# A fixed quarter of the experts as dense products beside the gathers

## The chip, the cores and the metric

The kernel runs on one core of a Trainium2 chip in one launch. The metric is the time of an execution on the device in microseconds (us). All values are 32-bit floats.

## The reference, cut to what matters

Two transformer layers run over 256 tokens of width 2048: a convolution block with a gated feed-forward, then attention, pooling and a mixture of single-neuron experts. The change touches only the mixture, the last part:

```python
q = (xt @ w_query).reshape(t, 8, 256); q1, q2 = halves of q
s1, s2 = q1 . sub_keys_1, q2 . sub_keys_2          # 128 keys each
v1, i1 = top_k(s1, 16); v2, i2 = top_k(s2, 16)
cand = v1[..., :, None] + v2[..., None, :]          # 16 x 16 pairs
top_s, pos = top_k(cand, 16); expert = i1 * 128 + i2 at pos
gates = softmax(top_s)
a = einsum('thkd,td->thk', expert_u[expert], x)     # 8 heads x 16 picks a token
hid = gelu(a) * gates
out = x_residual + einsum('thk,thkd->td', hid, expert_v[expert])
```

There are 128 x 128 = 16,384 experts. An expert's first key, 0 to 127, is its number divided by 128. The tables expert_u and expert_v have one row of 2048 floats (8 KB) for each expert.

## The kernel before, in words

The layers run stage by stage. Up to the query projection, weights stream in as 292 panels of 1 MB (128 partitions x 2048 floats) that SyncE (SP) loads into a ring of four buffers, `raw` (lines 364 to 369); ScalarE and VectorE split each panel into two parts, and TensorE (PE) multiplies.

The mixture starts when the last panel is used. Tokens lie on the partitions in two tiles of 128. A tile and a head make a *route* (16 routes), with 16 picks, in order of tile and head; four picks make a *group*, 64 groups in all (`ROUTES`, `GROUPS`, `BATCH`, lines 250, 251). One gather brings, for one pick of one route, one table row for each of the 128 partitions: 1 MB.

- **GpSimd (POOL)** issues the gathers in a fixed order: u of pick k, then v of pick k - 6 (`LAG`), as indirect DMAs (`gather_u`, line 441; `gather_v`, line 450). u has 4 buffers, and one comes free when the dot of four picks before is done. v has 8, and they come free four at a time, when TensorE has finished a group (`v_used`).
- **VectorE (DVE)** takes one dot per u buffer (`dot`, line 1282), its product going back into that buffer. Ahead of the third group of each route it works out the whole next route (`route`: the sixteen best keys of both halves, the best pairs, the expert numbers, the gates; lines 1221 to 1269). So a route is worked out in one group of four. After a group's four dots, `hidden` multiplies the activation by the gate.
- **ScalarE (ACT)** takes the gelu of four dots, writes `spread` (16 small copies of an identity, scaled by the hidden values, line 801) and copies each route's expert numbers into v's layout (16 copies, line 790).
- **TensorE** adds a group (`adds`, line 1646): 16 products of spread and v rows into four PSUM banks of the tile. Before the first and after the last group of a tile, `nothing` multiplies zeros (line 1634) to open and close the banks. VectorE then adds the banks to the residual (`result`, line 1322), and SP stores a tile (line 368).

The v rows lie differently from the u rows: partition 32 s + r of the buffer of pick 4 j + q holds token 32 q + r of pick 4 j + s.

```python
for k in range(ROUTES * TOPK + LAG):
    if k < ROUTES * TOPK:
        gather_u(k)
    if k >= LAG:
        gather_v(k - LAG)
```

Of the kernel before, what the change touches and what calls it, by code (L numbers as in the profile page):

```python
# [22 lines left out]
D = 2048  # L23
# [11 lines left out]
SLOTS = PH * TOPK  # L35
RMS_EPS, LN_EPS = 1e-6, 1e-5
# [77 lines left out]

class Counts:
# [39 lines left out]
def two_layers(nc, stream, columns, x, meta, b_out, g_mix_post, g_ffn_post, g_norm2, w_forget,  # L155
# [19 lines left out]

    cols = keep("s_cols", [128, NCOLS])
    ident = keep("s_ident", [128, 128])
    ones = keep("s_ones", [128, 128])
    tri_ones = keep("s_tri_ones", [128, 2 * 128])
    causal = keep("s_causal", [128, 128])  # L180
    group_sb = keep("s_group_w", [128, 4, 2, 256])
    wf_raw = keep("s_wf_raw", [128, KT, HEADS])
# [67 lines left out]
    NU, NV, NW, BATCH, LAG = 4, 8, 4, 4, 6  # L250
    ROUTES, GROUPS = TT * PH, TOPK // BATCH
    Q = 32
    u_slot = [place(f"s_u{i}", [128, D], ring0 + i * 8 * K) for i in range(NU)]
    v_slot = [place(f"s_v{i}", [128, D], ring0 + (NU + i) * 8 * K) for i in range(NV)]
    assert ring0 + (NU + NV) * 8 * K <= S
    P0 = S + 66 * K
    spread = [place(f"s_spread{i}", [128, 4, Q], P0 + i * 512) for i in range(NW)]
    P0 += NW * 512

    def small(name, n, dt=f32):  # L260
        nonlocal P0
        t = place(name, [128, n], P0, dt)
        P0 += (4 * n + 63) // 64 * 64
        return t

    sc = small("s_sc", 2 * NKEYS)
# [4 lines left out]
    cand = small("s_cand", TOPK * TOPK)  # L271
    cand_rest = small("s_cand_rest", TOPK * TOPK)
# [4 lines left out]
    pick = small("s_pick", TOPK * TOPK)  # L277
    chosen = small("s_chosen", 2 * TOPK)
    expert_f = [small(f"s_expert_f{i}", TOPK) for i in range(2)]
    u_index = [small(f"s_u_index{i}", TOPK, u32) for i in range(ROUTES)]  # L280
    v_index = [place(f"s_v_index{i}", [128, 4, GROUPS], S + 33 * K + i * 64, u32) for i in range(ROUTES)]
    gate = [small(f"s_pgate{i}", TOPK) for i in range(2)]
    gsum = small("s_gsum", 4)
    iota_i = small("s_iota_i", TOPK, mybir.dt.int32)
    iota_f = small("s_iota_f", TOPK)
# [3 lines left out]
    assert P0 <= S + 78 * K, P0 - S  # L289
    zeros = place("s_zeros", [128, 128], S + 65 * K)  # L290

    with ExitStack() as ctx:
# [41 lines left out]
        zeros_ready, iota_ready = sem("zeros_ready"), sem("iota_ready")  # L334
# [16 lines left out]
        def _(sp):  # L351
# [7 lines left out]
            with sp.Fori(1, NPANELS // 4) as q:  # L359
                for s in range(4):  # L360


                    sp.wait_ge(panel_used, q * 4 + (s - 4 + 1 + 1))
                    sp.dma_start(raw[s][:, :], panels[bass.ds(q, 1), s].rearrange("a p n -> (a p) n"))\
                        .then_inc(raw_loaded[s], 16)
            for t in range(TT):
                sp.wait_ge(out_ready, t + 1)
                sp.dma_start(out[t * 128:(t + 1) * 128, :], xres[:, t, :]).then_inc(stored, 16)
            sp.wait_ge(stored, 16 * TT)
# [3 lines left out]
        def _(pool):  # L373
# [7 lines left out]
            n.base["pool_step"] = 5  # L381
# [47 lines left out]
            pool.iota(iota_i[:, :], pattern=[[1, TOPK]], base=0, channel_multiplier=0).then_inc(iota_ready, 1)  # L429
            pool.memset(zeros[:, :], 0.0).then_inc(zeros_ready, 1)  # L430
# [4 lines left out]
            def gather_u(k):  # L435
# [5 lines left out]
                pool.indirect_dma_start(u_slot[k % NU][:, :], None, expert_u, index).then_inc(u_loaded[k % NU], 16)  # L441

            def gather_v(k):

                th, slot = divmod(k, TOPK)
                j, q = divmod(slot, 4)
                pool.wait_ge(v_index_ready, th + 1)
                wait(pool, v_used, (k - NV) // 4 + 1)
                index = bass.IndirectOffsetOnAxis(ap=v_index[th][:, q, j:j + 1], axis=0)
                pool.indirect_dma_start(v_slot[k % NV][:, :], None, expert_v, index).then_inc(v_loaded[k % NV], 16)  # L450
# [9 lines left out]
        def _(act):  # L460
# [321 lines left out]
            def route(th):  # L782

                act.wait_ge(gate_max, th + 1)
                act.activation(gate[th % 2][:, :], top[:, :], ACT.Exp, bias=gsum[:, 0:1], accum_out=gsum[:, 1:2])\
                    .then_inc(gate_exp, 1)
                act.wait_ge(expert_ready, th + 1)
                for s in range(4):
                    for q in range(4):
                        ins = act.activation(v_index[th][s * Q:(s + 1) * Q, q, :], expert_f[th % 2][q * Q:(q + 1) * Q, s::4], ACT.Copy)  # L790
# [13 lines left out]

            route(0)
            for g in range(ROUTES * GROUPS):
                th, j = divmod(g, GROUPS)
                if j == 2 and th + 1 < ROUTES:
                    route(th + 1)
                if g:  # L810
                    spreads(g - 1)
                part = slice(j * BATCH, (j + 1) * BATCH)
                act.wait_ge(dot_ready, (g + 1) * BATCH)
                act.activation(gelu[th % 2][:, part], adot[th % 2][:, part], ACT.Gelu_apprx_tanh).then_inc(gelu_ready, 1)  # L814
            spreads(ROUTES * GROUPS - 1)
# [3 lines left out]
        def _(dve):  # L819
# [412 lines left out]
            def best_keys(th, halves):  # L1232

                if 0 in halves:
                    link(dve.tensor_copy(sc[:, :], score[:, th, :]))
                for half in halves:
                    sixteen(val[:, half * TOPK:(half + 1) * TOPK], ind[:, half * TOPK:(half + 1) * TOPK],
                            sc[:, half * NKEYS:(half + 1) * NKEYS], sc_rest[:, :])
# [10 lines left out]
            def pairs_experts(th):  # L1249
# [5 lines left out]
                picks = pick[:, :].rearrange("p (k a) -> p k a", a=TOPK)  # L1255
                for half in range(2):
# [469 lines left out]
```

## Time and profile before

| | us |
|---|---|
| median of 3 runs | 3256.39 |
| lowest and highest | 3250.51, 3256.89 |
| the profiled execution | 3256.63 |
| its span, first to last instruction | 3254.9 |

The span has 38175 instructions. TensorE is busy for 68% of it, VectorE for 56%, ScalarE for 36%, GpSimd for 20%. Memory traffic is 855.36 MB, 543.27 of it on GpSimd's software queue and 310.85 on SP's hardware queue.

How to read it: times are microseconds from the start of the span, means of single instructions in nanoseconds. PE is TensorE's products and PEld its weight loads, which overlap them; a 32-bit product shows as two records. "Busy" is the union of an engine's instructions. Idle time is put down to what ended it (`<-`). PEclk is the granted share of TensorE's clock, and the DMA share is the mean busy share of 16 DMA engines. L1282 is line 1282 of the kernel.

### The profile page before, as it was taken

To read this page: it belongs to the slowest core of one execution; us is meant where nothing else is said; L and a number is where in the kernel's file an instruction comes from. 1 tells how busy PE (TensorE), PEld (TensorE's weight loads), DVE (VectorE), ACT (ScalarE), POOL (GpSimd) and SP (SyncE) were. 2 spreads that over 40 slices of the span, in tenths; PEclk is the share of its full clock that TensorE was granted. 3 is DMA by queue.
4 is the path that set the end of the run, shared out by engine and by line. 5 is a ranking of instruction groups with operands and counts; after the bars stand their busy time and mean duration, and the time that the engine had idled before them with its cause. 6 is when DMAs were issued, how large, how long until landed. Compare 5 with 4: busy or idle time off the path is not lost.

```text
span 3254.9 us, 38175 instructions
## 1 busy us (share of the span) xinstructions
PE 2201.9 (68%) x14110; PEld 1774.7 (55%) x14110; DVE 1827.5 (56%) x2515; ACT 1165.8 (36%) x2115; POOL 654.1 (20%) x557
## 2 busy tenths in 40 slices
PE   7996889999999969999999891222222232222324
PEld 6885679999999969889998780000000010000001
DVE  5896555555554553764445455555555565555553
ACT  2003354444444443344333443333333333333332
POOL 0000000000000000120000016444444444444442
PEclk9998989999999989899999996566666666666566
DMA  5331435555555535334555449999999999999998
GB/s 225 144 142 67 179 119 192 180 188 186 185 189 181 190 119 181 117 130 151 186 180 200 148 165 402 418 414 417 412 416 414 417 414 417 417 414 419 418 417 343
DMA packets 117560, 855.36 MB, mean 263 GB/s; under 512 B 13104, under 2 KB 13104, under 8 KB 13248
## 3 DMA queue, kind: packets, MB, share of 16 engines
q0 software_dynamic: 74656, 543.27, 40.6%
q1 hardware_dynamic: 42800, 310.85, 26.4%
q8 instruction: 47, 0.77, 0.1%
q14 instruction: 57, 0.47, 0.0%
HBM read 851.97 MB, written 2.10 MB: 262 GB/s over the span
## 4 chain that ended last, share of the span: by engine, by line
PE 50%; DMA 21%; DVE 14%; issue 6%; POOL 5%; ACT 3%; DVEq 0%; POOLq 0%; SPq 0%; ACTq 0%
DMA s_u<-in_expert_u,s_u_index 19%; PE bank L1355 13%; PE bank L1357 13%; PE bank L1356 13%; PE bank L1435 7%; DVE s_u L1282 4%; POOL s_u L441 3%; POOL s_v L450 2%; DMA s_v<-in_expert_v,s_v_index 2%; DVE s_w_lo L842 1%; DVE s_yrow L1008 1%; PE bank L1646 1%; ACT s_w_hi L471 1%; DVE s_qrs L1046 1%; ACT s_xs L477 0%
## 5 line engine op out<-in xcount | busy, mean ns | idle before, releaser
L1646 PE MATMUL bank<-s_v,s_spread 128*32 128x512 f32 x2048 | 368.3, 884 | 922.9 <-DMA s_v<-in_expert_v,s_v_index 907.8
L842 DVE TENSOR_TENSOR s_w_lo<-s_raw,s_w_hi 128x2048 fp32r<-128x2048 f32 x259 | 594.7, 2297 | 646.8 <-ACT s_w_hi L471 646.6
L1282 DVE CUSTOM_DVE_ANT_0 s_u<-s_u,s_xn 128x2048 f32<-128x2048 f32 x256 | 584.1, 2291 | 505.6 <-DMA s_u<-in_expert_u,s_u_index 505.0
L1646 PEld LDWEIGHTS bank<-s_v,s_spread 128*32 128x32 f32 x2048 | 93.0, 155 | 1197.9 <-issue 1037.5
L471 ACT ACTIVATE s_w_hi<-s_raw 128x2048 fp32r<-128x2048 f32 x260 | 497.8, 1915 | 652.5 <-PE bank L1357 652.4
L1355 PE MATMUL bank<-s_a_hi,s_w_hi 128*128 128x256 f32 x2560 | 722.5, 282 | 12.8 <-DVE s_w_lo L842 7.8
L1356 PE MATMUL bank<-s_a_lo,s_w_hi 128*128 128x256 f32 x2560 | 722.7, 282 | 0.0
L1357 PE MATMUL bank<-s_a_hi,s_w_lo 128*128 128x256 f32 x2560 | 722.0, 282 | 0.0
L1355 PEld LDWEIGHTS bank<-s_a_hi,s_w_hi 128*128 128x128 f32 x2560 | 486.1, 190 | 17.5 <-DVE s_w_lo L842 10.5
L1357 PEld LDWEIGHTS bank<-s_a_hi,s_w_lo 128*128 128x128 f32 x2560 | 486.8, 190 | 0.0
L1356 PEld LDWEIGHTS bank<-s_a_lo,s_w_hi 128*128 128x128 f32 x2560 | 482.9, 189 | 1.4 <-issue 1.0
L441 POOL DMA_INDIRECT s_u<-in_expert_u,s_u_index x256 | 320.0, 1250 | 773.7 <-DVE s_adot L1282 510.0
L801 ACT ACTIVATE s_spread<-s_ident,s_hid 32x32 f32<-32x32 f32 x1024 | 325.5, 318 | 218.0 <-DVE s_hid L1291 205.6
L450 POOL DMA_INDIRECT s_v<-in_expert_v,s_v_index x256 | 297.2, 1161 | 95.8 <-issue 79.4
L408 POOL MEMSET s_pin<- 128x128 f32 x1 | 0.2, 207 | 1367.6 <-ACT s_pin L603 1367.6
L1435 PE MATMUL bank<-s_a_f,s_raw 128*128 128x272 f32 x1024 | 236.6, 394 | 0.8 <-DVE s_a_f L889 0.8
L1435 PEld LDWEIGHTS bank<-s_a_f,s_raw 128*128 128x128 f32 x1024 | 195.6, 191 | 41.5 <-DVE s_a_f L889 0.9
L916 DVE SCALAR_TENSOR_TENSOR s_cacc<-s_cvg,s_cols,s_cacc 128x256 f32<-128x256 f32 x464 | 185.9, 478 | 0.8
L814 ACT ACTIVATE s_gelu<-s_adot 128x4 f32<-128x4 f32 x64 | 13.1, 205 | 478.8 <-DVE s_adot L1282 478.6
L1355 PE MATMUL bank<-s_w_hi,s_a_hi 128*128 128x512 f32 x320 | 131.0, 409 | 24.7 <-DVE s_w_lo L842 11.5
L1355 PE MATMUL bank<-s_w_hi,s_h_hi 128*128 128x512 f32 x352 | 137.3, 390 | 0.0
L1357 PE MATMUL bank<-s_w_hi,s_h_lo 128*128 128x512 f32 x352 | 137.2, 390 | 0.0
(266 smaller groups left out, 2293.2 us busy)
## 6 DMA issues: line engine op xcount, KB each, us to landing
s_raw<-in_stream SPq DMA_DIRECT2D x292, 1024.0 KB, 4.8
s_u<-in_expert_u,s_u_index POOLq DMA_INDIRECT x256, 16.5
s_v<-in_expert_v,s_v_index POOLq DMA_INDIRECT x256, 17.9
s_xres<-in_x SPq DMA_DIRECT2D x2, 1024.0 KB, 7.1
out<-s_xres SPq DMA_DIRECT2D x2, 1024.0 KB, 6.5
s_bout_row<-in_b_out POOLq DMA_DIRECT2D x1, 1024.0 KB, 9.2
s_gmix_row<-in_g_mix_post POOLq DMA_DIRECT2D x1, 1024.0 KB, 12.7
s_gffn_row<-in_g_ffn_post POOLq DMA_DIRECT2D x1, 1024.0 KB, 17.2
```

Source lines behind the costliest of these rows:

```text
L441: pool.indirect_dma_start(u_slot[k % NU][:, :], None, expert_u, index).then_inc(u_loaded[k % NU], 16)
L450: pool.indirect_dma_start(v_slot[k % NV][:, :], None, expert_v, index).then_inc(v_loaded[k % NV], 16)
L471: act.activation(w_hi[s % 2][:, :], raw[s][:, :], ACT.Copy).then_inc(hi_ready, 1)
L801: ins = act.activation(spread[g % NW][s * Q:(s + 1) * Q, q, :], ident[own, own], ACT.Copy, scale=hid[th % 2][own, 4 * j + s:4 * j + s + 1])
L842: dve.tensor_tensor(w_lo[s % 2][:, :], raw[s][:, :], w_hi[s % 2][:, :].bitcast(f32), ALU.subtract)\
L916: step(dve.scalar_tensor_tensor(acc, u, w, acc, ALU.mult, ALU.add))
L1282: dve.tensor_tensor_reduce(out=u_slot[k % NU][:, :], in0=u_slot[k % NU][:, :], in1=xn[:, th // PH, :], scale=1.0, scalar=0.0, op0=ALU.mult ...
L1355: pe.matmul(dst, left[0], right[0], start=start, stop=False)
L1356: pe.matmul(dst, left[0], right[1], start=False, stop=False)
L1357: return pe.matmul(dst, left[1], right[0], start=False, stop=stop)
L1435: ins = pe.matmul(bank[c][:, 0:L], raw[c % 4][:, k * 128:(k + 1) * 128], a_f[:, k, :], start=k == 0, stop=k == KT - 1)
L1646: ins = pe.matmul(bank[4 * t + c][q * Q:(q + 1) * Q, :], spread[g % NW][:, q, :], v_slot[(4 * g + q) % NV][:, c * 512:(c + 1) * 512], star ...
```

## The change

The experts whose first key is 0 to 31 (`DENSE` = 32, 4,096 of 16,384) are computed for all 256 tokens. The tables of these experts come as 32 u panels (laid out on the host in a new input `dense_u`, 2048 features on the partitions) and 32 v panels (rows of `expert_v` as they are), 1 MB each, which SP loads after the weight panels into two buffers. TensorE multiplies each u panel with the tokens, ScalarE takes the gelu into `ha` (32 tiles of 128 experts x 256 tokens). The gates of these experts come as products of two one-hot tiles for each token: VectorE compares 128 slots with the numbers 0 to 127 (second key) and with 0 to 31 (first key, times the gate); TensorE's product of both is the token's 128 x 32 table of gates, 16 tokens to a bank; VectorE multiplies it into `ha`. The v panels are then multiplied with `ha` into the same banks as the gathered experts.

In the gathers, these experts get a number past the table (2 x 16,384 is added), and the indirect DMAs have a bounds check that skips them; their gate is zero (`gate_kept`), and the buffer holds what was there.

The order of the work changes: `route` is cut into four pieces, one behind each dot of a group, and routes 1 to 15 are worked out in four groups of five (`route_in`), in groups 0 to 17. The u panels stand in steps 1 to 21 of TensorE's loop (1.5 a step, then two in 18 to 21), the one-hot tokens in groups 20 to 30, the v panels in steps 34 to 59; TensorE's step i does the panels first and then the adds of group i - 2. The v buffers are 7 (`NV`), the dot writes one common tile and waits for the dot before, and the residual enters the banks as products with the identity instead of zeros; the last copies and stores run by banks.

```diff
+def route_in(g):
+    return g - g // 5 + 1 if g % 5 < 4 and g - g // 5 + 1 < TT * PH else None
+def u_panels_in(i):
+    if 1 <= i <= 16:
+        return range(3 * (i - 1) // 2, 3 * i // 2)
+    return range(24 + 2 * (i - 18), 26 + 2 * (i - 18)) if 18 <= i < 22 else range(0)
+def token_fours_in(g, turn):
+    if 20 <= g < 22:
+        return range(4 * (g - 20) + turn, 4 * (g - 20) + turn + 1)
+    z = 4 * (g - 22) + turn
+    return range(8 + 56 * z // 36, 8 + 56 * (z + 1) // 36) if 22 <= g < 31 else range(0)
+def v_panels_in(i):
+    return range(5 * (i - 34) // 4, min(DENSE, 5 * (i - 33) // 4)) if i >= 34 and 5 * (i - 34) // 4 < DENSE else range(0)
...
-    NU, NV, NW, BATCH, LAG = 4, 8, 4, 4, 6
+    NU, NV, NW, BATCH, LAG = 4, 7, 4, 4, 6
...
+            for d in range(2 * DENSE):
+                sp.wait_ge(panel_used, NPANELS + 1 + d + 1 - (2 if d >= 2 else 4))
+                src = dense_u[d] if d < DENSE else expert_v[(d - DENSE) * NKEYS:(d - DENSE + 1) * NKEYS, :]
+                sp.dma_start(raw[d % 2][:, :], src).then_inc(raw_loaded[d % 2], 16)
...
-                pool.indirect_dma_start(u_slot[k % NU][:, :], None, expert_u, index).then_inc(u_loaded[k % NU], 16)
+                pool.indirect_dma_start(u_slot[k % NU][:, :], None, expert_u, index, bounds_check=NKEYS * NKEYS - 1,
+                                        oob_is_err=False).then_inc(u_loaded[k % NU], 16)
...
+                if k == 0:
+                    pool.wait_ge(res_taken, 1)
+                    pool.wait_ge(xnt_ready, 1)
                 wait(pool, v_used, (k - NV) // 4 + 1)
...
+            def dense_hidden(d):
+                b = 4 + d % 2
+                act.wait_ge(panel_used, NPANELS + 1 + d + 1)
...
+                act.activation(ha[:, dense_block(d), :], bank[b][:, 0:T], ACT.Gelu_apprx_tanh).then_inc(bank_empty[b], 1)
...
+                step(dve.tensor_scalar(kept[:, :], key[0], float(DENSE), None, ALU.is_ge))
+                step(dve.tensor_scalar(dense_f[:, :], key[0], float(DENSE), float(2 * NKEYS * NKEYS), ALU.is_lt, ALU.mult))
...
                 dve.wait_ge(u_loaded[k % NU], (k // NU + 1) * 16)
-                dve.tensor_tensor_reduce(out=u_slot[k % NU][:, :], in0=u_slot[k % NU][:, :], in1=xn[:, th // PH, :],
+                wait(dve, dot_ready, k)
+                dve.tensor_tensor_reduce(out=product_out[:, :], in0=u_slot[k % NU][:, :], in1=xn[:, th // PH, :],
...
+            def one_keys(f):
...
+                wait(dve, one_key_used, f - 1)
+                for token in range(4 * f, 4 * f + 4):
+                    column = slots_t[token // 128][:, token % 128:]
+                    own, own_2 = slice(token % 8 * NKEYS, (token % 8 + 1) * NKEYS), slice(token % 8 * DENSE, (token % 8 + 1) * DENSE)
+                    dve.tensor_scalar(one_key[:, own], iota_f[:, :], column[:, SLOTS:SLOTS + 1], None, ALU.is_equal)
+                    ins = dve.tensor_scalar(one_key_2[:, own_2], iota_f[:, 0:DENSE], column[:, 0:1], column[:, 2 * SLOTS:2 * SLOTS + 1],
+                                            ALU.is_equal, ALU.mult)
...
+            def gated(group):
...
+                dve.wait_ge(one_key_used, 4 * (group + 1))
+                some = ha[:, :, 16 * group:16 * (group + 1)]
+                dve.tensor_tensor(some, some, bank[b][:, :].rearrange("p (t g) -> p g t", t=16), ALU.mult).then_inc(bank_empty[b], 1)
...
+            dve.wait_ge(panel_used, NPANELS + 1)
+            for half in range(2):
+                some = slice(half * 8, (half + 1) * 8)
+                ins = dve.tensor_tensor(xnt[:, some, 0:T], a_hi[:, some, 0:T].bitcast(f32), a_lo[:, some, 0:T].bitcast(f32), ALU.add)
...
             for g in range(ROUTES * GROUPS):
...
+                for turn in range(BATCH):
+                    dot(g * BATCH + turn)
+                    if turn == 0 and g:
+                        hidden(g - 1)
+                        if route_in(g - 1):
+                            gates_softmax(route_in(g - 1))
+                    if route_in(g):
+                        route(route_in(g), turn)
+                    for f in token_fours_in(g, turn):
+                        if f >= 8 and f % 4 == 0:
+                            gated(f // 4 - 2)
+                        one_keys(f)
...
+            def residual(t):
                 for c in range(4):
+                    ins = pe.matmul(bank[4 * t + c][:, :], ident[:, :], xres[:, t, c * 512:(c + 1) * 512], start=True, stop=False)
...
+            def dense_u_panel(d):
+                b = 4 + d % 2
...
+                for k in range(KT):
+                    ins = pe.matmul(bank[b][:, 0:T], raw[d % 2][:, k * 128:(k + 1) * 128], xnt[:, k, 0:T], start=k == 0, stop=k == KT - 1)
+                ins.then_inc(panel_used, 1)
...
+            def dense_v_panel(d):
...
+                for t in range(TT):
+                    for c in range(4):
+                        ins = pe.matmul(bank[4 * t + c][:, :], ha[:, d, t * 128:(t + 1) * 128], raw[d % 2][:, c * 512:(c + 1) * 512],
+                                        start=False, stop=d == DENSE - 1 and t == 0)
...
+            def token_four(f):
...
+                for token in range(4 * f, 4 * f + 4):
...
+                    ins = pe.matmul(bank[b][:, token % 16 * DENSE:(token % 16 + 1) * DENSE], one_key[:, own], one_key_2[:, own_2],
+                                    start=True, stop=True)
...
+            for i in range(ROUTES * GROUPS + 2):
+                for d in u_panels_in(i):
+                    dense_u_panel(d)
...
+                for d in v_panels_in(i):
+                    dense_v_panel(d)
+                if i >= 2:
+                    adds(i - 2)
+                for turn in range(BATCH):
+                    for f in token_fours_in(i, turn):
+                        token_four(f)
```

## Rows read from the trace of the kernel before

**Rows 1.** Page, slices: busy tenths and granted clock in 40 slices of the span.

```profile
PE   7996889999999969999999891222222232222324
...
PEclk9998989999999989899999996566666666666566
DMA  5331435555555535334555449999999999999998
```

**Rows 2.** Stretches of the gather stage (columns: the row of names).

```profile
core 0: us, PE busy (x) PEld busy (x) DVE busy (x) ACT busy (x) POOL busy (x), PEclk, DMA share, GB/s
...
2300.00:2600.00 300.00, 86.16 (x480) 21.70 (x480) 173.21 (x282) 103.12 (x334) 144.13 (x120) 0.64 1.01 414
...
2900.00:3200.00 300.00, 86.38 (x480) 21.86 (x480) 168.16 (x261) 98.14 (x315) 136.67 (x121) 0.63 1.01 419
```

**Rows 3.** DMA queues and issues, 1960 to 3200 us.

```profile
q0 software_dynamic: 70503, 513.42, 100.4%
...
s_u<-in_expert_u,s_u_index POOLq DMA_INDIRECT x248, 16.5
s_v<-in_expert_v,s_v_index POOLq DMA_INDIRECT x247, 18.0
```

**Rows 4.** Waits from 1960 us on: us in total, times, longest.

```profile
PE bank L1646 <- DMA s_v<-in_expert_v,s_v_index: 907.8, 63, 34.3
DVE s_u L1282 <- DMA s_u<-in_expert_u,s_u_index: 503.6, 190, 4.7
POOL s_u L441 <- DVE s_adot L1282: 502.1, 136, 12.3
...
POOL s_v L450 <- PE bank L1646: 16.4, 12, 9.1
```

**Rows 5.** Page, DMA issues: weight panels, median us to landing.

```profile
s_raw<-in_stream SPq DMA_DIRECT2D x292, 1024.0 KB, 4.8
```

**Rows 6.** Timeline, first gather and the end of the span.

```profile
1935.01 1.03 POOL L441 DMA_INDIRECT s_u<-in_expert_u,s_u_index  x1 [194.55 <-PE bank L1357]
...
3239.08 5.34 PE L1646 MATMUL bank<-s_v,s_spread 128*32 128x512 f32 x32 [4.21 <-DMA s_v<-in_expert_v,s_v_index]
...
3244.35 3.70 PE L1634 MATMUL bank<-s_xn,s_zeros 128*128 128x512 f32 x8
```

**Rows 7.** Groups of instructions by line, VectorE.

```profile
L1282 DVE CUSTOM_DVE_ANT_0 s_u<-s_u,s_xn 128x2048 f32<-128x2048 f32 x256 | 584.1, 2291 | 505.6 <-DMA s_u<-in_expert_u,s_u_index 505.0
...
L1258 DVE TENSOR_TENSOR s_pick<-s_iota_f,s_posf 128x256 f32<-128x256 f32 x32 | 13.6, 425 | 1.1
...
L1322 DVE TENSOR_TENSOR s_xres<-s_xres,bank 128x512 f32<-128x512 f32 x8 | 5.0, 680 | 23.8 <-PE bank L1634 23.8
...
L1269 DVE TENSOR_SCALAR s_pgate<-s_pgate,s_gsum 128x16 f32<-128x16 f32 x16 | 3.8, 234 | 0.6
...
L1253 DVE TENSOR_SCALAR s_pos<-s_pos 128x16 uint32<-128x16 uint32 x16 | 2.7, 168 | 0.0
```

**Rows 8.** Timeline, VectorE's first copy of a route and the dot behind it.

```profile
2617.16 0.29 DVE L1235 COPY s_sc<-s_score 128x256 f32<-128x256 f32 x1
...
2629.40 2.29 DVE L1282 CUSTOM_DVE_ANT_0 s_u<-s_u,s_xn 128x2048 f32<-128x2048 f32 x1
```

**Rows 9.** Timeline, two gather issues of GpSimd.

```profile
2604.34 0.94 POOL L450 DMA_INDIRECT s_v<-in_expert_v,s_v_index  x1 [0.30 <-issue]
...
2632.47 2.32 POOL L441 DMA_INDIRECT s_u<-in_expert_u,s_u_index  x1 [12.28 <-DVE s_adot L1282]
```

**Rows 10.** TensorE: two groups by line, then timeline of adds and ScalarE's spreads.

```profile
L1435 PE MATMUL bank<-s_a_f,s_raw 128*128 128x272 f32 x1024 | 236.6, 394 | 0.8 <-DVE s_a_f L889 0.8
...
L1612 PE MATMUL bank<-s_keys,s_qp 128*128 128x128 f32 x64 | 7.6, 277 | 0.5 <-ACT s_qp L603 0.5
...
2602.43 5.27 ACT L801 ACTIVATE s_spread<-s_ident,s_hid 32x32 f32<-32x32 f32 x16 [4.85 <-DVE s_hid L1291]
...
2607.63 5.86 PE L1646 MATMUL bank<-s_v,s_spread 128*32 128x512 f32 x32 [14.54 <-DMA s_v<-in_expert_v,s_v_index]
```

More of the change, by code:

```diff
@@ L35 @@
 SLOTS = PH * TOPK
+DENSE = 32
 RMS_EPS, LN_EPS = 1e-6, 1e-5
@@ L807, in _ @@
                 th, j = divmod(g, GROUPS)
-                if j == 2 and th + 1 < ROUTES:
-                    route(th + 1)
+                if g == 20:
+                    for t in range(TT):
+                        slots_transposed(t)
                 if g:
                     spreads(g - 1)
+                    for d in u_panels_in(g - 1):
+                        dense_hidden(d)
                 part = slice(j * BATCH, (j + 1) * BATCH)
@@ L1255, in pairs_experts @@
                 picks = pick[:, :].rearrange("p (k a) -> p k a", a=TOPK)
+                key = [picked[th // PH][:, half * SLOTS + th % PH * TOPK:][:, 0:TOPK] for half in range(2)]
                 for half in range(2):
                     part = slice(half * TOPK, (half + 1) * TOPK)
-                    link(dve.tensor_tensor(picks, iota_f[:, :].unsqueeze(1).to_broadcast(square),
+                    link(dve.tensor_tensor(picks, iota_f[:, 0:TOPK].unsqueeze(1).to_broadcast(square),
                                            posf[:, part].unsqueeze(2).to_broadcast(square), ALU.is_equal))
@@ L1278, in dot, with route @@
+            def route(th, turn):
+                if turn < 2:
+                    best_keys(th, turn)
+                elif turn == 2:
+                    best_pairs()
+                else:
+                    pairs_experts(th)
             def dot(k):
@@ new lines, in dense_v_panel @@
+            def dense_v_panel(d):
+                pe.wait_ge(raw_loaded[d % 2], (NPANELS // 4 + (DENSE + d) // 2 + 1) * 16)
+                for t in range(TT):
+                    for c in range(4):
+                        ins = pe.matmul(bank[4 * t + c][:, :], ha[:, d, t * 128:(t + 1) * 128], raw[d % 2][:, c * 512:(c + 1) * 512],
+                                        start=False, stop=d == DENSE - 1 and t == 0)
+                        if d == DENSE - 1 and t == 0:
+                            ins.then_inc(acc_done, 1)
+                ins.then_inc(panel_used, 1)
@@ new lines, in slots_transposed @@
+            def slots_transposed(t):
+                pe.wait_ge(gates_ready, PH * (t + 1))
+                into(6 + t, 0)
+                for kind in range(3):
+                    ins = pe.transpose(bank[6 + t][:, kind * SLOTS:(kind + 1) * SLOTS], picked[t][:, kind * SLOTS:(kind + 1) * SLOTS], ident[:, :])
+                ins.then_inc(bank_full[6 + t], 1)
+            def token_four(f):
+                b = 6 + f // 4 % 2
+                if f % 4 == 0:
+                    into(b, 1 + f // 8)
+                pe.wait_ge(one_key_ready, f + 1)
+                for token in range(4 * f, 4 * f + 4):
+                    own, own_2 = slice(token % 8 * NKEYS, (token % 8 + 1) * NKEYS), slice(token % 8 * DENSE, (token % 8 + 1) * DENSE)
+                    ins = pe.matmul(bank[b][:, token % 16 * DENSE:(token % 16 + 1) * DENSE], one_key[:, own], one_key_2[:, own_2],
+                                    start=True, stop=True)
+                ins.then_inc(one_key_used, 1)
```

198 lines of the change are left out of this document (118 added, 80 removed).

## The prediction, on record before the changed kernel was run

> **What bounds the kernel now.** I read the slices of the page first, then the gather stage in stretches, then the waits, then single instructions. In the slices [rows 1] the DMA row reads 9 from the 25th slice to the last but one, while TensorE reads 2 or 3 and its clock mostly 6: the last 40% of the span are bounded by transfers. The stretches of this stage [rows 2] say the same: a DMA share of 1.01 at 414 to 419 GB/s, VectorE busy for 168 to 173 of 300 us, TensorE for 86. Nearly all of it is the gathers' software queue [rows 3], 100.4% of 16 engines. The stage runs from the first gather at 1935.0 us to the last adds at 3239.1 [rows 6]: 1304 us for 512 gathers of 128 rows of 8 KB, so 2.54 us each, and 20.3 us for a group (four u and four v). A row thus takes one DMA engine 2.54 / 8 = 0.32 us. The waits [rows 4] agree: TensorE waits 907.8 us for v rows, VectorE 503.6 for u rows, and GpSimd 502.1 us for a dot to free a u slot; the ring of v slots costs only 16.4. Some seven gathers are in flight: each lands 16.5 to 18.0 us after its issue [rows 3].
>
> **What the change does to the transfers.** A row whose expert's first key is below 32 is out of bounds and, if the instruction does what it says, is not fetched. I counted the reference's own routing for its inputs (a count, no time): 74.6% of the 65,536 rows stay, 72.2% in the first 18 groups, 76.0% in groups 34 to 59. Evenly spread, the gathers would need 0.746 x 1302 = 971 us. 64 panels of 1 MB come back, each 128 rows as well: 64 x 2.54 = 163 us. An even sum would be 1134 against 1302, a gain of 168 us. Two things stand against it.
>
> **First, the rows that stay are not even.** The granularity is one engine's eight of the 128 rows. A token's picks share few first keys, so that whole stretches of one engine's rows vanish while another's stay. Counting with a fixed assignment by partition, tried in three ways, the fullest engine holds 78 to 79% of a full load over the whole stage, 81 to 83% summed over windows of 64 gathers, 85 to 88% over windows of eight. A gather is done when its fullest engine is, and seven are in flight [rows 3], so the price lies between 0.75 (no imbalance) and 0.88. I take 0.82, the windows of 64: an engine that falls behind may stay behind through several windows, but passing from one late engine to another skips the gathers in flight. A group then needs 0.82 x 20.3 = 16.7 us, plus 2.54 us for each panel in it. That is 19.7 to 19.8 with the 1.2 v panels a group of groups 34 to 59. The trace can't show which engine carries which row. The Trainium skill (DMA: Bandwidth & Descriptors, "The descriptor swizzle") states that in a 1 MB software-queue transfer the partition fixes the engine, eight partitions each; by it the loss stands, and without it the first rival below is what happens. No row here decides it.
>
> **Second, VectorE.** Dense gates need every route known, so routes 1 to 15 move from one in four groups to four in five, all in groups 0 to 17. The route in the timeline takes 12.2 us from its first copy to the next dot [rows 8]; it loses the 0.29 us copy and gains four small instructions of some 0.17 each (the smallest of [rows 7]), partly overlapped: 12.4. A dot takes 2.29 [rows 7] and now waits for the one before, as all write one tile; I add 0.16, a small instruction's length, for read-out and hop, so 9.8 us a group. Bounds of that wait: 0 and 0.3. A group with a route costs VectorE 9.8 + 0.2 + 12.4 = 22.4 us, more than before's 20.3 from transfers. The fifth group has none and runs by the transfers, some 17: a mean of 21.3.
>
> Groups 20 to 30 carry the one-hot tokens: 256 tokens with two comparisons each (128 and 32 wide). No row has these. Width costs (425 - 168) / 240 = 1.07 ns an element, a scalar from memory 66 ns more than a constant (234 against 168) [rows 7], so 0.35 and 0.25 us if nothing overlaps, 0.17 together if only the widths count; they are issued without links, so I take 0.42 a token, nearer the upper end. 25 tokens a group give 10.5 us; the gating products read PSUM at 0.68 [rows 7], 1.6 a group: 1.1. Sum 9.8 + 0.2 + 1.1 + 10.5 = 21.6 us, bounds 16.7 (transfers) to 26.
>
> **TensorE** has room. A u panel is 32 passes; one of width 272 takes 236.6 / 1024 = 0.231 us [rows 10], so 7.0 us at full clock; a v panel is 16 passes at 3.70 / 8 = 0.46 [rows 6]: 7.4. The adds take 5.9 [rows 10], at the lower of the clock's two levels (0.64 granted on average [rows 2]). 1.5 u panels and adds make 16.4 us, under 21.3; a u step of two panels 19.9, and with 16 tokens (two passes each, 7.6 / 64 = 0.12 us a pass [rows 10]) 23.6 in groups 20 and 21. If the clock stayed at 1.2 GHz a u panel would cost 14; I don't expect it beside 80% busy, since the stretch of [rows 1] in which TensorE reads 9 has clock 9. ScalarE's spreads are 5.27 us a group [rows 10]; one or two dense activations more and the moved index copies are hidden under 20.
>
> **Queues passed.** SP idles in this stage; its 64 panel issues wait for the panel two back, and a panel lands in 4.8 us when alone [rows 5]. Nothing waits behind them but the output. GpSimd's issue is 0.94 us when VectorE idles and 2.32 when it starts under a dot [rows 9]; eight a group are 8 to 18 us, hidden under 20, but without slack where VectorE never rests. It also waits on two new events before the first v row (the residual's products and the transposed tokens, two VectorE adds of about 2.3): both end before the first v gather's turn, which before came after six u gathers. Cost nothing; if the cover is gone, 5 us. One v slot goes (8 to 7): below.
>
> **Ends.** The closing zero products (3.7 us, [rows 6]) go, and copies and stores run by banks of 512: -6 us, bounds -9 and 0.
>
> **Sum**, in us against 20.34 a group before: groups 0 to 17, 18 x 21.3 = 384 (366); 18 to 21, with two u panels each, 4 x 22.3 = 89 (81); 22 to 30, 9 x 21.6 = 194 (183); 31 to 33, 3 x 16.7 = 50 (61); 34 to 59, 26 x 19.8 = 515 (529); 60 to 63, 67 (81). That is 1299 against 1302, so -3, and the ends -6: 9 us off. The profiled execution took 3256.6 (span 3254.9), which is the median of the runs shown (3256.4) within 0.3 us: **3247 us**. What the transfers save at the end is spent by VectorE in front.
>
> **Rivals.**
> *The rows are even after all* (descriptors dealt out after the skip, or the backlog smooths them). For: the share of 1.01 leaves no gap that uneven engines would show, though nothing was uneven then. Groups 34 to 59 fall to 0.76 x 20.34 + 3.1 = 18.6, 31 to 33 to 15.1, 60 to 63 to 14.9, 18 to 21 to 20.5; the front keeps 20.8 by VectorE, 22 to 30 their 21.6. Sum 483 + 45 + 60 + 82 + 375 + 194 = 1239: 63 less, with the ends 69: 3188 us.
> *The v ring of seven decides* (slower). The last v row of a group may be issued only when all adds of the group before are done, since those hold four slots and the other three are taken. The loop is adds 5.9 + hop 0.3 + issue 0.94 + landing. It decides above a landing of 20.3 - 7.1 = 13.2 us; the landings now are 18.0 [rows 3], but eight slots let it span two groups, and only 16.4 us are waited [rows 4]. With fewer rows a landing shortens; alone it is far less. At 14 us the 42 groups from 22 on take 21.1 each, 886 against the 826 above: +60, 3308 us. For it: the stretch in which GpSimd waits also narrows the window, and the imbalance is then nearer 0.88.
> *The skip saves no traffic* (each row still costs a packet): 163 us of panels come on top, 3256.6 + 163 - 6 = 3414 us.
>
> **Chances.** My forecast 0.37, even rows 0.25, the v ring 0.28, no skip 0.04, others 0.06 (one-hot comparisons dear or cheap, TensorE held at 1.2 GHz). The measurement can tell about 0.2% from no change, 3249.9 to 3262.9. The forecast lies just below that band, its own range (0.79 to 0.86 for the imbalance, 17 to 24 us in groups 22 to 30) is 3205 to 3290. Faster: 0.37 x 0.5 + 0.25 + 0.01 = 0.45; same: 0.37 x 0.3 + 0.02 = 0.13; slower 0.42. The range 3170 to 3325 holds the forecast, even rows and most of the ring; it leaves out no skip and the far ends.
>
> **What would show it.** Right: in groups 34 to 59 a DMA share of 0.95 at 385 to 390 GB/s with VectorE waiting for u rows; in groups 0 to 17 VectorE busy over 90% and some 350 GB/s; the software queue at 405 MB, the hardware queue at 378. Even rows would show as a share of 1.00 and over 410 GB/s in groups 34 to 59 at 18.6 us a group; the ring as GpSimd waiting for the adds for hundreds of us. I am wrong if groups 0 to 17 run under 20 us, if TensorE's panels end the waits, or if the software queue still moves 543 MB.

## The result and the profile after

The changed kernel takes 3306.49 us (median of 4 runs, 3300.26 to 3311.43) beside 3255.57 for the kernel before: a ratio of 1.0158, 95% interval 1.0135 to 1.0181. It is slower by 51 us; the forecast was 9 us faster. The profiled execution took 3300.26 us, its span is 3298.5.

The slices of the page, beside [rows 1]: TensorE now reads 5 to 7 in the gather stage, and the DMA row, all nines before, has sevens and eights up to the 32nd slice.

```profile
PE   8997799999999979899999866776677656767663
...
DVE  5896455555555553854454477867649964444454
...
PEclk9998999999999989999999987888886678888887
DMA  5332445555555534334545467888878899999998
```

The page's DMA part. Before, the software queue had the same 74656 packets with 543.27 MB, and 13104 packets of all queues were under 512 B:

```profile
DMA packets 127667, 786.29 MB, mean 238 GB/s; under 512 B 30898, under 2 KB 30898, under 8 KB 32066
...
q0 software_dynamic: 74656, 406.74, 32.2%
q1 hardware_dynamic: 52880, 377.97, 31.3%
```

The bytes are as forecast (405 and 378 MB): the skip does what it says. The packets under 512 B are 17,794 more. That is 16,674 skipped rows (25.44% of 65,536) and 16 closing packets for each of the 64 panels and the 6 more output stores: 1,120. So a skipped row leaves a packet of 4 bytes in the queue; those packets show a median of 9 ns, against 309 to 312 ns for a row of 8 KB.

Stretches of the changed kernel, cut at the first dot of groups 0, 18, 22, 31, 34 and 60 (beside [rows 2]):

```profile
core 0: us, PE busy (x) PEld busy (x) DVE busy (x) ACT busy (x) POOL busy (x), PEclk, DMA share, GB/s
1938.00:2348.00 410.00, 268.24 (x1331) 187.52 (x1330) 316.63 (x836) 192.25 (x615) 195.52 (x142) 0.82 0.84 321
2348.00:2458.00 110.00, 74.99 (x403) 55.60 (x401) 50.15 (x104) 28.25 (x92) 45.70 (x32) 0.84 0.79 309
2458.00:2650.00 192.00, 132.00 (x736) 88.77 (x736) 180.81 (x544) 48.30 (x155) 95.14 (x74) 0.66 0.86 305
...
2697.00:3206.00 509.00, 353.86 (x1343) 128.98 (x1341) 241.34 (x235) 137.57 (x442) 318.89 (x209) 0.86 0.97 388
```

The same cuts in the kernel before and in all runs give the table by which everything below is read. A stretch runs from the start of its first dot to the start of the next stretch's; the last ends with the last dot. All in us, from the profiled executions.

| groups | before | after | change | forecast | adds_first | act_first | no_one_hot | even_skip | ring_six | four_tokens | lag_five |
|---|---|---|---|---|---|---|---|---|---|---|---|
| 0 to 17 | 361.5 | 409.3 | +47.8 | +18 | 362.7 | 381.1 | 363.0 | 359.9 | 443.7 | 365.6 | 367.2 |
| 18 to 21 | 80.7 | 110.0 | +29.3 | +8 | 99.7 | 87.1 | 80.3 | 93.2 | 109.9 | 94.4 | 91.6 |
| 22 to 33 | 242.6 | 239.7 | -2.9 | 0 | 238.1 | 236.1 | 209.0 | 234.0 | 242.9 | 213.6 | 209.1 |
| 34 to 59 | 517.1 | 508.5 | -8.6 | -14 | 510.6 | 511.2 | 509.8 | 470.3 | 548.9 | 510.8 | 508.7 |
| 60 to 63 | 77.4 | 66.9 | -10.5 | -14 | 66.9 | 68.8 | 66.5 | 61.1 | 76.2 | 65.1 | 65.2 |

The first dot starts 6.2 us earlier than before and the end after the last dot is 5.4 us shorter, -11.6 where -6 was forecast. The 5.4 us are the forecast's ends; the 6.2 are not to be told from chance, since the first dot starts anywhere from 1938.4 to 1946.7 us in the traces of all these kernels. The sum is 43.6 us but for rounding, the difference of the two spans. Of the 53 us between forecast and profiled execution, 51 lie in groups 0 to 21, where the u panels stand.

What holds these groups is in the waits from 1960 to 2340 us (us in total, times, longest):

```profile
PE bank L1767 <- ACT s_ha L873: 134.4, 14, 37.3
POOL s_v L511 <- PE bank L1810: 66.9, 8, 15.5
...
DVE s_product_out L1370 <- DMA s_u<-in_expert_u,s_u_index: 39.5, 14, 6.3
...
PE bank L1810 <- DMA s_v<-in_expert_v,s_v_index: 7.4, 1, 7.4
```

VectorE, which was to be the bound here, is busy for 316.6 of 410 us, 77%, and waits for u rows for only 39.5. TensorE waits 134.4 us for a dense activation of ScalarE, and GpSimd 66.9 us for TensorE's adds; before, it waited 16.4 us over the whole stage [rows 4]. The timeline of one step shows the order of it (start, length, engine, line, idle time before and what ended it):

```profile
2144.30 5.27 ACT L863 ACTIVATE s_spread<-s_ident,s_hid 32x32 f32<-32x32 f32 x16
...
2149.59 1.28 ACT L873 ACT_TABLE_LOAD   x1
...
2150.89 0.66 ACT L873 ACTIVATE s_ha<-bank 128x256 f32<-128x256 f32 x2
...
2151.32 9.50 PE L1767 MATMUL bank<-s_xnt,s_raw 128*128 128x256 f32 x32 [11.33 <-ACT s_ha L873]
...
2160.75 3.64 PE L1810 MATMUL bank<-s_v,s_spread 128*32 128x512 f32 x32
...
2165.28 2.21 POOL L511 DMA_INDIRECT s_v<-in_expert_v,s_v_index  x1 [9.29 <-PE bank L1810]
```

ScalarE does 16 spreads (5.27 us), loads its table (1.28) and only then takes the two dense activations that free the banks; TensorE has stood 11.33 us for the first of them. It runs a u panel (9.50), and behind it the adds. The adds are those of the group two steps back: their spreads had been ready for a group, and they start right behind the panel, with no wait for their v rows. The adds free the v buffers for which GpSimd has waited 9.29 us with a v gather, and every u gather stands behind that in its queue.

The wait also makes the panel itself longer. TensorE stopped at 2140.0 us, its granted clock was 0.51 (the lower level, 1.2 GHz) from 2142 to 2156 us, and the panel took 9.50 us; of the 32 u panels 17 took 7.1 to 7.2 us and 15 took 8.7 to 10.1. In adds_first, described below, only three took over 7.2.

In groups 18 to 21 there is a second loop. VectorE may write the one-hot tiles of four tokens only when TensorE has multiplied those of two fours before, and these products stand behind the u panels and the adds of their step. From 2348 to 2458 us:

```profile
DVE s_one_key L1383 <- PE bank L1797: 30.1, 2, 19.2
```

### The profile page after: what moved, and what is told of

Its sections match the earlier page's. It is cut to its first block and busy times, and to the rows that moved or that the text cites. A ratio compares the mean times of both kernels' runs of the same rounds, so it can differ in the third digit from the quotient of the medians.

```text
span 3298.5 us, 43743 instructions
## 1 busy us (share of the span) xinstructions
PE 2704.9 (82%) x16148; PEld 2151.2 (65%) x16148; DVE 1947.9 (59%) x3093; ACT 1177.7 (36%) x2149; POOL 786.6 (24%) x557
## 3 DMA queue, kind: packets, MB, share of 16 engines
q0 software_dynamic: 74656, 406.74, 32.2%
## 5 line engine op out<-in xcount | busy, mean ns | idle before, releaser
L1370 DVE CUSTOM_DVE_ANT_0 s_product_out<-s_u,s_xn 128x2048 f32<-128x2048 f32 x256 | 586.4, 2291 | 401.8 <-DMA s_u<-in_expert_u,s_u_index 377.3
L511 POOL DMA_INDIRECT s_v<-in_expert_v,s_v_index x256 | 418.5, 1635 | 376.6 <-PE bank L1810 186.6
L1810 PE MATMUL bank<-s_v,s_spread 128*32 128x512 f32 x2048 | 307.6, 755 | 240.9 <-DMA s_v<-in_expert_v,s_v_index 240.9
L498 POOL DMA_INDIRECT s_u<-in_expert_u,s_u_index x256 | 331.1, 1293 | 426.1 <-PE bank L1479 195.8
L1767 PE MATMUL bank<-s_xnt,s_raw 128*128 128x256 f32 x1024 | 259.5, 418 | 162.0 <-ACT s_ha L873 162.0
L1810 PEld LDWEIGHTS bank<-s_v,s_spread 128*32 128x32 f32 x2048 | 77.6, 134 | 447.7 <-issue 374.6
L1767 PEld LDWEIGHTS bank<-s_xnt,s_raw 128*128 128x128 f32 x1024 | 215.0, 212 | 214.6 <-ACT s_ha L873 173.1
L1775 PE MATMUL bank<-s_raw,s_ha 128*128 128x512 f32 x512 | 226.6, 597 | 0.0
```

Source lines behind the costliest of these rows:

```text
L1370: dve.tensor_tensor_reduce(out=product_out[:, :], in0=u_slot[k % NU][:, :], in1=xn[:, th // PH, :], scale=1.0, scalar=0.0, op0=ALU.mult, o ...
L1767: ins = pe.matmul(bank[b][:, 0:T], raw[d % 2][:, k * 128:(k + 1) * 128], xnt[:, k, 0:T], start=k == 0, stop=k == KT - 1)
L1810: ins = pe.matmul(bank[4 * t + c][q * Q:(q + 1) * Q, :], spread[g % NW][:, q, :], v_slot[(4 * g + q) % NV][:, c * 512:(c + 1) * 512], star ...
```

## The experiments

Times are medians; the ratio (with its 95% interval) is to the kernel before, timed beside it on the same chip.

### Are the rows' DMA engines fixed? (skip_low8, skip_mod4, skip_real)

All three are the kernel before with bounds-checked gathers, and the products of the dots in two tiles of their own; nothing dense is computed. They differ in what is out of bounds:

```diff
+ skip_low8:  skip_f = 2 * NKEYS * NKEYS where (partition & 31) < 8
+ skip_mod4:  skip_f = 2 * NKEYS * NKEYS where (partition & 3) == 0
+ skip_real:  skip_f = 2 * NKEYS * NKEYS where the first key < 32
+                link(dve.tensor_tensor(expert_f[th % 2][:, :], expert_f[th % 2][:, :], skip_f[:, :], ALU.add))
```

> The kernel before, with a quarter of the gathered rows out of bounds in every gather: those of the partitions whose number modulo 32 is below 8, whatever their expert. Nothing dense is computed, so the output lacks these picks. If a row's DMA engine is fixed by its partition, in blocks of four partitions, four engines get no rows and twelve all of theirs: each gather still takes 2.54 us and the time stays at 3250 to 3260 us. If the rows left are dealt out evenly, the 1304 us of the gather stage fall by up to a quarter: 2930 us, or 3050 if GpSimd and VectorE become the limit.

> As skip_low8, but the quarter left out is every fourth partition (number modulo 4 is 0), which takes two of eight rows from every engine under a fixed assignment by blocks of four. Nothing dense is computed. Both theories expect the same here: the stage falls by up to a quarter, to 2930 us; between 2930 and 3050 if GpSimd's issues and the dots become the limit. The difference to skip_low8 is the price of imbalance alone, at equal bytes. If a skipped row cost as much as a fetched one, the time would stay at 3255 us.

> The kernel before, with the rows of experts whose first key is below 32 out of bounds (25.4% of them), and nothing dense computed in their place. Fixed engines: the factor on the 1304 us lies where the prediction put it, 0.82 (0.79 to 0.87), so 3020 us (2980 to 3085), clearly above skip_mod4. Even rows: as skip_mod4 within 10 us.

Measured: skip_low8 3255.75 us (0.9993, 0.9983 to 1.0003), skip_mod4 3074.92 (0.9442, 0.9427 to 0.9458), skip_real 3138.65 (0.9632, 0.9616 to 0.9648).

A quarter of the bytes less gave nothing in the first and 184 us in the second; the queue of skip_low8 moved 409 MB. Its page's queue and its stretch from 2000 to 3000 us, where the DMA share was 1.01 before:

```profile
q0 software_dynamic: 74656, 409.11, 30.8%
```

```profile
2000.00:3000.00 1000.00, 286.38 (x1592) 72.94 (x1584) 577.69 (x963) 334.61 (x1074) 487.82 (x397) 0.64 0.76 312
```

A share of 0.76 at 312 GB/s, and the gathers no faster: this is what twelve of sixteen engines at work all the time and four with hardly anything to do would give (the trace doesn't name the engine of a row). With skip_mod4, which is faster at equal bytes, it shows that a row's engine goes by its partition and that nothing is dealt out again. That the blocks are of four partitions is not shown: blocks of eight neighbours would give the same in both runs. The Trainium skill (DMA: Bandwidth & Descriptors, "The descriptor swizzle") gives blocks of four for a 1 MB transfer; the two runs agree with it for indirect gathers with rows left out.

skip_mod4 fell short of the 326 us of an even quarter, and of my 3050:

```profile
2000.00:3000.00 1000.00, 338.93 (x1856) 86.36 (x1848) 674.35 (x1126) 390.22 (x1253) 723.73 (x461) 0.65 0.92 364
```

```profile
POOL s_u L447 <- ACT s_v_index L798: 139.9, 14, 12.1
```

The share is 0.92. In these 1000 us GpSimd waits 14 times, up to 12.1 us, before a u gather. The line names ScalarE's copies, which end at the same time, but `gather_u` waits for no copy: what it waits for is a u buffer, freed by the first dot behind a route, as in [rows 9]. The route is worked out in one piece, and the shorter backlog of faster gathers (a v row lands 8.4 us after its issue, 18.0 before [rows 3]) no longer covers its 12 us. The real rows cost 64 us more than the even ones, and skip_real's 3139 us lie outside the 2980 to 3085 that I expected. So the imbalance is shown, but its size here is blurred by the route's stop, which both have. In the changed kernel the route is cut into four pieces; what that alone does to the stop no run shows.

### What holds groups 0 to 21? (adds_first, act_first)

```diff
 adds_first, TensorE's step i:            act_first, ScalarE's group g:
+    adds(i - 2)                          +    dense_hidden of the panels of g - 1
     dense_u_panel / dense_v_panel             spreads(g - 1)
-    adds(i - 2)                          -    dense_hidden of the panels of g - 1
```

> The changed kernel, where TensorE in each step does the adds of the gathered group first and the dense panels after them (nothing else is moved). Theory A, that the adds queue behind u panels which wait for a bank that ScalarE frees, and with them the v ring, GpSimd and the u rows: groups 0 to 21, 519 us now, fall by 40 to 60 us, the time to 3245 to 3265 us, and TensorE's wait for the dense activation no longer delays GpSimd. Theory B, that VectorE's routes and the transfers themselves fill these groups: no change beyond 10 us, 3295 to 3305 us.

> The changed kernel in its own order on TensorE (panels ahead of adds), where ScalarE in each group takes the dense activations first and the 16 spreads after them, so that a bank for the next u panel is free about 5.3 us earlier. If the adds are late because the panel ahead of them waits for that bank, groups 0 to 21 (519 us) give back a part of what adds_first gave back (57 us): 15 to 40 us, 3265 to 3290 us. If only the 7 to 14 us of the panels' own products delay the adds, nothing changes: 3295 to 3310 us.

Measured: adds_first 3252.92 us (0.9984, 0.9972 to 0.9997), act_first 3254.54 (0.9999, 0.9989 to 1.0008). Either swap of order alone takes back the whole loss, with the same work and bytes. In adds_first groups 0 to 17 fall by 46.6 us and 18 to 21 by 10.3; in act_first by 28.2 and 22.9, more than I had expected. All other groups stay within 4 us. The waits of adds_first from 1960 to 2340 us:

```profile
PE bank L1810 <- DMA s_v<-in_expert_v,s_v_index: 83.9, 11, 30.8
...
PE bank L1767 <- ACT s_ha L873: 22.0, 7, 8.0
...
POOL s_v L511 <- PE bank L1810: 19.2, 7, 4.6
```

TensorE's wait for the activation is 22.0 us (134.4 in the changed kernel), GpSimd's for the adds 19.2 (66.9), and what ends TensorE's idle time is the landing of v rows. In act_first the same two waits are:

```profile
PE bank L1767 <- ACT s_ha L873: 116.5, 15, 32.0
...
POOL s_v L511 <- PE bank L1810: 85.5, 11, 10.7
```

Their sums hardly fall there, and GpSimd's even rises, while the time falls by as much. So the sum of a wait is no price of it. What act_first changes is when the panel, and the adds behind it, may start: no longer after the spreads of the newest group. Theory B is refuted, but VectorE is the next bound: in adds_first it is busy for 87% of this stretch (first row; the next two are of groups 22 to 30 and 34 to 59).

```profile
1945.00:2305.00 360.00, 249.46 (x1288) 167.96 (x1290) 313.20 (x830) 189.43 (x600) 185.31 (x142) 0.86 0.95 366
...
2420.00:2590.00 170.00, 118.28 (x667) 79.97 (x667) 165.48 (x498) 42.37 (x136) 89.36 (x67) 0.66 0.88 307
2700.00:3100.00 400.00, 278.48 (x1043) 100.60 (x1041) 188.02 (x183) 107.41 (x345) 244.32 (x162) 0.85 0.97 391
```

In adds_first a group with a route takes 21.2 us as a rule, the three without one (4, 9 and 14) take 11.6 to 13.5, and the group behind such a one 21.0 to 25.3. In the changed kernel the three take 22.5, 19.2 and 24.0 us, and 28.8 of the 46.6 us of difference are theirs: VectorE sets 21.2 us in many of the others in both kernels, and the late adds cost most where it could have caught up.

In groups 18 to 21 adds_first still takes 19.0 us more than the kernel before. VectorE's wait for the one-hot products is still 28.0 us there (2305 to 2405 us), beside 30.1 in the changed kernel.

### What do the one-hot tokens cost? (no_one_hot)

```diff
 on top of adds_first
-                    for f in token_fours_in(g, turn): gated(...), one_keys(f)     # VectorE
-                    for f in token_fours_in(i, turn): token_four(f)               # TensorE
```

> The kernel adds_first without the one-hot tokens: no comparisons, no products for them, no gating of the dense activations (so the dense experts enter without their gates). Theory: in groups 20 to 30 VectorE is the bound through 256 x 0.40 us of comparisons; without them these groups fall from 21.3 us to the transfers' 17 us, and the group that waits for the transposed slots (24 to 39 us) comes down too: 45 to 60 us less than adds_first, 3195 to 3210 us. Rival: the u panels of steps 18 to 21 and the products on TensorE hold these groups: less than 20 us, 3235 us or more.

Measured: 3200.30 us (0.9812, 0.9796 to 0.9828), 53 us under adds_first. Groups 18 to 21 fall from 99.7 to 80.3 and 22 to 33 from 238.1 to 209.0. The stretch 2420 to 2590 us of this kernel, beside the second row above:

```profile
2420.00:2590.00 170.00, 59.71 (x324) 15.02 (x321) 92.86 (x90) 52.96 (x170) 140.27 (x81) 0.63 0.97 371
```

VectorE's share falls from 97% (165.48 of 170) to 55%, the DMA share rises from 0.88 to 0.97. This run takes away TensorE's products as well; that VectorE's comparisons are the bound in groups 22 to 33 is shown by four_tokens below, which keeps the products. In groups 18 to 21 the tokens cost 19.4 us by VectorE's wait for these products, so there the rival has its share. The comparisons (least, median, longest ns, starts) of the changed kernel:

```profile
L1383 DVE TENSOR_SCALAR s_one_key<-s_iota_f,s_slots_t x256: 267/274/486, 2391.2 to 2649.3; 128x128 f32<-128x128 f32 x128
L1384 DVE TENSOR_SCALAR s_one_key<-s_iota_f,s_slots_t x256: 281/290/527, 2391.4 to 2649.6; 128x32 f32<-128x32 f32 x128
```

Nearly 0.29 us each, and in the timeline they start 0.20 us apart: 0.40 us a token, 0.42 in the prediction.

### What do the uneven rows cost in the changed kernel? (even_skip)

```diff
 on top of adds_first: the rows of every fourth partition are out of bounds, not those of the dense experts
-    dense_f = 2 * NKEYS * NKEYS where key[0] < DENSE
+    dense_f = 2 * NKEYS * NKEYS where (partition & 3) == 0
```

> The kernel adds_first, where the rows left out are those of every fourth partition instead of those of the dense experts (the same share, spread evenly over the DMA engines; the output is wrong in the picks left out). The difference to adds_first is the price of the uneven rows inside the changed kernel. By the runs without dense work (skip_real 64 us above skip_mod4 over 512 gathers) I expect half of it in groups 31 to 63, where the transfers bound, and little before: 25 to 40 us less, 3210 to 3230 us, groups 34 to 59 at 18.5 to 18.9 us each. If the panels fill the gaps of the idle engines, no more than 10 us.

Measured: 3192.86 us (0.9791, 0.9775 to 0.9807), 60 us under adds_first, more than the 25 to 40 that I expected, 40 of them in groups 34 to 59. The stretch 2700 to 3100 us, beside the third row above:

```profile
2700.00:3100.00 400.00, 299.43 (x1143) 109.25 (x1141) 203.08 (x199) 116.42 (x374) 267.53 (x175) 0.88 1.02 416
```

1.02 and 416 GB/s against 0.97 and 391. A group takes 18.09 us against 19.64. Taking off 1.23 panels of 2.54 us leaves 15.0 and 16.5 us for eight gathers, against 19.9 in the kernel before: factors of 0.75 and 0.83. Of the difference 0.01 is no imbalance: 75% of the rows are fetched there in even_skip and, by the count in the prediction, 76.0% in adds_first. So the panels fill the gaps of the idle engines for the DMA share, but not for the clock on the wall: a gather still waits for its fullest engine.

### Does the ring of v buffers decide? (ring_six, lag_seven, lag_five)

```diff
 ring_six, on top of the changed kernel      NU, NV, NW, BATCH, LAG = 4, 6, 4, 4, 6
 lag_seven, on top of four_tokens (below)    NU, NV, NW, BATCH, LAG = 4, 7, 4, 4, 7
 lag_five, on top of four_tokens             NU, NV, NW, BATCH, LAG = 4, 7, 4, 4, 5
```

> The changed kernel with six v buffers instead of seven; nothing else. If the loop over the v ring (adds of a group, issue, landing, adds of the next) sets the pace wherever no dense u panel stands in front of the adds, one slot less bites at once: groups 34 to 59, 19.6 us each, go to 21 or more, and the whole to 3350 us or above. If the ring is short only because the adds stand behind the u panels (groups 0 to 21), those groups lose another 20 to 40 us and groups 34 to 59 stay within 0.4 us of 19.6: 3320 to 3345 us.

> The kernel four_tokens with the v gathers one pick further behind the u gathers (lag 7 instead of 6), so that the v row that waits for the ring stands behind one more u gather. Ring theory: GpSimd waits there for the adds (93.5 us in all) with u gathers queued behind it, and the window of transfers in flight narrows; one more u gather ahead shortens that wait and gives 5 to 20 us, 3205 to 3220 us. Rival: v rows then land later, the adds are later by as much, and the time is 3220 to 3230 us.

> The kernel four_tokens with lag 5 instead of 6. Lag 7 cost 23 us there, most of it in groups 18 to 30, with later v rows. If late v rows are what costs, lag 5 gives 3200 to 3218 us; if lag 6 already balances them against GpSimd's wait for the ring, which now stands one u gather earlier, the time goes up again: 3230 to 3250 us.

Measured: ring_six 3400.11 us (1.0416, 1.0383 to 1.0449); lag_seven 3246.78 (0.9972, 0.9962 to 0.9983); lag_five 3214.31 (0.9862, 0.9842 to 0.9882). With six buffers groups 34 to 59 go to 21.1 us each, as the first theory said, groups 0 to 17 lose another 34 us, and GpSimd's wait for the adds in groups 34 to 59 doubles. The first row is ring_six (2745 to 3285 us), the second the changed kernel (2700 to 3200 us):

```profile
POOL s_v L511 <- PE bank L1810: 143.7, 20, 11.2
```

```profile
POOL s_v L511 <- PE bank L1810: 68.4, 16, 7.7
```

With seven the ring still costs some waiting, but groups 34 to 59 run at the pace of the uneven rows, as even_skip shows by going to 18.09 with the same ring. No run has eight buffers: there was no room. The lag, which I had expected to help by growing, hurt at seven (0.9972 against four_tokens' 0.9891) and helped a little at five (0.9862). The interval of lag_five overlaps four_tokens' own, but beside both_orders below (lag 6, timed together with it) each of its executions is faster: 3211.97 to 3215.41 us against 3217.56 to 3225.12. From 1960 to 3200 us TensorE waits 264, 291 and 347 us for v rows at lag 5, 6 and 7, and VectorE 28.6, 54.8 and 81.2 us for the one-hot products, which stand behind the adds in TensorE's step; GpSimd's wait for the adds hardly moves (97.3, 93.5 and 102.0). So late v rows reach VectorE through TensorE's order; that this is all of the difference is not shown.

### A faster version (four_tokens, both_orders)

```diff
 four_tokens, on top of adds_first
+    transposes of the slots ahead of the u panels of step 19; one-hot tokens in groups 20 to 32
-    8 x tensor_scalar on one token                   # for four tokens
+    tensor_tensor is_equal on [128, 4, 32]; is_equal on [128, 4, 128]; mult on [128, 4, 32]
 both_orders, on top of four_tokens: ScalarE's order of act_first as well
```

> A version meant to be faster: adds_first; the transposes of the slots ahead of the u panels of their step; the one-hot tiles of four tokens compared in three wide instructions instead of eight, spread over groups 20 to 32 instead of 20 to 30. By the rows of the changed kernel eight comparisons start every 0.20 us, 1.6 us for four tokens; three wide ones are about 0.95 (512 elements at 1.07 ns, two of 128). VectorE's sum in groups 22 to 32 falls below the transfers' 17 us: 3205 to 3225 us. If the comparisons were not the bound there, 3245 us or more.

> The kernel four_tokens, in which ScalarE also takes the dense activations ahead of the spreads. The two orders helped in different groups: TensorE's took 47 us from groups 0 to 17 and 10 from 18 to 21, ScalarE's 28 and 23. Together, groups 0 to 17 stay at 363 to 366 us (VectorE's 22 us a group with a route are the bound there), groups 18 to 21 fall from 94 to 82 to 88 us: 3212 to 3220 us. If the bank's wait is the same time seen twice, nothing is left to gain: 3221 to 3227 us.

Measured: four_tokens 3223.92 us (0.9891, 0.9875 to 0.9908), both_orders 3221.82 (0.9887, 0.9870 to 0.9905). Groups 22 to 33 of four_tokens are within 5 us of those without any one-hot work (213.6 and 209.0), with all of TensorE's products in place. ScalarE's order adds nothing that can be measured, and groups 18 to 21 stay at 97.7 us where I expected 82 to 88: the bank's wait was the same time seen twice, the rival of my expectation. The best version is lag_five, 1.4% faster than the kernel before and 2.9% faster than the changed one. Its stretch 2420 to 2590 us shows a DMA share of 0.96, for 0.88 in adds_first:

```profile
2420.00:2590.00 170.00, 125.74 (x722) 79.02 (x722) 148.71 (x256) 52.94 (x170) 142.84 (x79) 0.68 0.96 359
```

## Why the prediction was wrong

**The step that failed** is "TensorE has room", with ScalarE's dense activations "hidden under 20". I added the engine's busy time in a step (16.4 us, and 23.6 in groups 20 and 21) and compared it with the group. The engine had that room: 74.99 of 110 us busy even where a group took longest. But it works in order, and its step puts u panels ahead of adds. The panel's wait for a bank hangs on ScalarE, whose activation stands behind the spreads of the group: 134.4 us from 1960 to 2340 us, which my sum held at nothing. What is queued behind the waiting panel is the adds, behind them the v ring, GpSimd and all u gathers. That TensorE's panels end the waits stood among my signs of being wrong, but neither the sum nor a rival had a price for it. The price of the order is 57 us by adds_first and 51 by act_first (groups 0 to 21). Against the forecast, groups 0 to 17 are 30 us over and groups 18 to 21 are 21 over; of these 21 adds_first gives back 10, and the rest goes with the one-hot tokens (no_one_hot: 80.3 us), whose products VectorE awaits behind the same panels. For groups 18 to 21 I had put 22.3 us a group without a working: transfers give 16.7 + 5.1 = 21.8 by my own figures.

**Right, point by point.** The bytes; the ends (5.4 us for 6); the u panel at full clock (7.0 against 7.1); the cost of a token (0.42 against 0.40 us) and groups 22 to 33 (0 forecast, -2.9 measured), bound by VectorE up to group 30. The factor of uneven rows, 0.82 between 0.75 and 0.88: 0.83 by even_skip, and that the partition decides is shown by skip_low8 and skip_mod4. So the rival of even rows is refuted (3188 us; even_skip, which makes them even, takes 3193 with the order mended). That a skip saves no traffic is refuted. Groups 34 to 59 had 388 GB/s, as forecast, at a share of 0.97 for my 0.95. The signs for groups 0 to 17 failed: VectorE was busy for 77%, not over 90, at 321 GB/s for 350; with the order mended it is 87% and 366.

**Right in the sum only.** The rival of the v ring gave 3308 us, and 3306.5 came out, but by another way, which is luck: its place was groups 22 to 63, priced at 886 us, and they took 815. Its mechanism is real one buffer further down: ring_six has 21.1 us a group in groups 34 to 59.

**Off in size, and luck again.** A group with a route takes VectorE 21.2 us, not 22.4, and the fifth group 11 to 14, not 17: adds_first has 362.7 us in groups 0 to 17 against 384 forecast. A group of groups 34 to 59 took 19.9 us before, not 20.34, as the 1304 us hold the start and end of the stage as well, so less was saved there. With the order right the sum would have come out nearly true, 7.7 us off the span for 9, by errors that cancel: +1.2 us for +18 in groups 0 to 17, +19.0 for +8 in 18 to 21, -6.5 for -14 in 34 to 59.

## What to carry to other kernels

An engine's sum of busy times says nothing of its order: for each instruction put ahead of others, ask what it waits for, and follow what stands behind it through the buffers to the queue that bounds. Rows left out of a gather save time only as far as every DMA engine loses the same share; count the fullest engine over some windows before counting bytes. A stage bound by transfers hides lumps of work by its backlog, and faster transfers shorten just that cover.

## What the runs showed of the hardware that I had not expected

A row out of bounds still leaves a packet of 4 bytes, of 9 ns: the number of packets of the software queue stays at 74656 to the last one. With the rows of 8 in every 32 partitions left out, the engines that still have all of theirs are no faster: the 312 GB/s of skip_low8 are three quarters of the 416 before (2000 to 3000 us), at the same time.
